# Two blocks made one, a hand-over reordered, and a two-instruction final normalisation in a one-core encoder kernel

## Chip, cores and metric

The kernel runs on one core of a Trainium2 chip. The metric is the device time of one execution in microseconds (us), lower is better. Engines are named as in the profile: PE is TensorE's matrix multiplication, PEld its weight loads, DVE is VectorE, ACT is ScalarE, POOL is GpSimd, SP is SyncE, which here only issues DMAs.

## The reference

One layer of a hybrid encoder on 16 meta tokens and 512 frames of 1024 channels, in float32:

```
h = layernorm(concat(meta, x))
p = h @ w_in                     # one projection, split among the branches
A = sparse attention: top-k keys by an indexer, attention in a 128-wide latent
    (q_abs = q . w_uk, softmax over the chosen keys, o_lat . w_uv)
B = RWKV-7 time mixing: a delta-rule scan over the tokens, 8 heads of 64
h = layernorm(alpha*h + (sigmoid(gA) * (A @ w_pa) + sigmoid(gB) * (B @ w_pb)) @ w_o)
q = h @ peer_wq                  # 8 heads x 2 halves of 128
experts = top 16 of 128 x 128 product keys per head, gates = softmax of the 16 scores
h = layernorm(alpha*h + sum over experts of gate * gelu(h . u[e]) * v[e])
```

## The kernel before

The program is a row of stages, each a block in which every engine has its own queue; engines meet by semaphores. Between two blocks all engines meet at a barrier, and the stage's semaphores are cleared.

- `project` (to about 326 us of the profile): the input norm, the projection, the choice of keys.
- `attend` (328 to 412): SP loads w_uk and w_uv at the block's start. PE turns the latent keys (line 968), multiplies the queries of eight heads by w_uk (line 976; ACT copies each result to q_abs, line 919), then for four query tiles of 128: scores (988), softmax by DVE and ACT, transposes of the probabilities (999), latent sums (1008), and `attended_of` (1017), whose result ACT copies in `take_out` (941). POOL builds the seven masks of the scan.
- `scan_chunks` (412 to 560): SP loads w_pa. DVE makes scaled keys (`make_hats`, 1166), PE turns values and keys (`turn`, 1283), then products of keys and queries (`gram`, 1299), steps of a triangular inverse (1320), and so on, for one tile of 16 tokens and four of 128.
- `join` and `peer` share one last block, from 561 us on. `join` mixes the branches and multiplies by w_o (line 1581): for each of NT = 4 tiles of 128 tokens two halves of 512 channels. DVE adds each half to h_tok (1650), takes moments (1654, 1656), ACT a root (1519, `root_of`), DVE normalises (1660). PE turns the tile before last (`turn`, 1559), ACT and DVE copy it to h1T (1528, 1636), ACT makes the high parts h_hl (1533, 1535), DVE the low parts (1643). High and low parts are the two pieces by which a float32 product is done as three fp32r products.
- `peer` streams tiles of 128 columns of weights: ACT makes the high part of each (`high`, line 1960 in the loop of heads), POOL the low part (`low`, line 1938), PE multiplies. The first two tiles are the queries of head 0; they are done in halves of 256 tokens (`query_half`, 2066 and 2070). Later tiles have 384 or 512 tokens (`tile`, 2083 and 2087). DVE ranks scores (lines 2220 to 2265) and makes gates (2273 to 2284), which PE turns (2137). POOL's queue begins with a wait for the last w_o product.
- Tokens of tiles 1 to 3 go densely through all 128 experts of each of 128 key rows (EXPERT_KEYS = 128): hidden values (2083, 2087), gelu (2040), gates (2345), high and low coefficients (2034, 2349), sums with v in PSUM (2177). The last HLS = 3 key rows are summed tile by tile. Tile 0 is gathered instead: 2 x PICKS = 256 gathered row sets, which DVE multiplies (1687) and adds (1696) between its other work; the last one is added in the turn of key row 124.
- After the loop over key rows, DVE finishes each tile: adds PSUM (2391), moments (2394, 2396), ACT's root (2050), reciprocal (2376), subtract and scale (2378), times g2 (2381), plus b2 (2383); SP stores it (1927). SP loads the rows g2 and b2 (1923, 1924) once the last low part is made.

Of the kernel before, what the change touches and what calls it, by code (L numbers as in the profile page):

```python
# [22 lines left out]
ALU = mybir.AluOpType  # L23
# [94 lines left out]
def build(nc, a, out):  # L118

    with ExitStack() as ctx:  # L120
# [17 lines left out]
        eps = sb("eps", [P, 4])  # L138

# [8 lines left out]
        with ExitStack() as layer:  # L148
# [9 lines left out]
            masks = sb("masks", [P, 7, CHUNK], at=layer)  # L158
            project(nc, a, locals())
            attend(nc, a, locals())  # L160
            w_pa = sb("w_pa", [P, PAIRS, D], at=layer)
            scan_chunks(nc, a, locals())
# [16 lines left out]
def project(nc, a, g):  # L179
# [19 lines left out]
    with ExitStack() as ctx:  # L199
# [53 lines left out]
        wi_summed, wi_taken = sem("wi_summed"), sem("wi_taken")  # L253
# [17 lines left out]
        def _(sp):  # L271
# [553 lines left out]
def attend(nc, a, g):  # L825


# [4 lines left out]
    with ExitStack() as ctx:  # L832
        sb = lambda name, shape: ctx.enter_context(nc.sbuf_tensor(name, shape, F32))
        sem = semaphores(nc, ctx, "attend")
        w_uk = sb("w_uk", [P, PAIRS, KV])
        w_uv = sb("w_uv", [P, HEADS * HD])
        cT, c_tok = p_all[:, CT_CKV, 1:PW], sb("c_tok", [P, 1 + NT, KV])
        q_abs = sb("q_abs", [P, HEADS, SEQ])
        probs = sb("prob", [P, 2, HEADS, T])
        peak, low_peak, total, share = (sb(n, [P, HEADS]) for n in ("peak", "low_peak", "total", "share"))  # L840
        probT = sb("probT", [P, 3, 4 * P])
        lat = sb("lat", [P, HEADS, P])
        landed = sem("uk_landed")
        c_turned, c_copied, abs_done, abs_copied = sem("c_turned"), sem("c_copied"), sem("abs_done"), sem("abs_copied")
        att_done, att_read, exped, shared, scaled_s, scaled_v = (
            sem(n) for n in ("att_done", "att_read", "exped", "shared", "scaled_s", "scaled_v"))
        turned, turn_copied, lat_copied, out_done, out_copied = (
            sem(n) for n in ("p_turned", "p_copied", "lat_copied", "oa_done", "oa_copied"))
        order_sem = sem("dve_order2")
        q = p_all[:, CT_Q:CT_Q + 4, 1 + META:PW]  # L850
        ones, masks = g["ones"], g["masks"]
        whole = [sb(f"mask{n}", [P, P]) for n in range(6)]
        pool_order, used = sem("pool_order4"), sem("probT_used")

        turns_before = lambda i: sum(2 * (x + 2) for x in range(i))
        units = lambda i: 2 * (i + 2)

        def heads_at(i, u):

            return range(HEADS * u // units(i), HEADS * (u + 1) // units(i)) if i + 1 < NT else range(0)  # L860

        block = ctx.enter_context(nc.Block())

        @block.sync
        def _(sp):
            sp.dma_start(w_uk[:, :, :], a["w_uk"]).then_inc(landed, 16)
            sp.dma_start(w_uv[:, :], a["w_uv"]).then_inc(landed, 16)
            sp.wait_ge(landed, 32)

        @block.gpsimd  # L870
        def _(pool):

            order = Order(pool, pool_order)
            below16, below32, below64, above16, above64, upto64 = whole

            def within(dst, w):
                view = dst[:, :].rearrange("p (b w) -> p b w", w=w)
                order.put(nc.gpsimd.affine_select(out=view, in_=ones[:, :].rearrange("p (b w) -> p b w", w=w),
                                                  compare_op=ALU.is_ge, fill=0.0, base=0,
                                                  pattern=[[-w, P // w], [0, w]], channel_multiplier=1))  # L880
                order.settle()
                order.put(nc.gpsimd.affine_select(out=view, in_=view, compare_op=ALU.is_ge, fill=0.0, base=w - 1,
                                                  pattern=[[w, P // w], [0, w]], channel_multiplier=-1))

            def side(dst, src, mult, strict):

                return nc.gpsimd.affine_select(out=dst[:, :], in_=src[:, :], compare_op=ALU.is_ge, fill=0.0,
                                               base=-strict, pattern=[[mult, P]], channel_multiplier=-mult)

            within(above16, 16)  # L890
            within(above64, 64)
            within(below32, 32)
            order.settle()
            order.put(nc.gpsimd.tensor_tensor(below64[:, :], above64[:, :], below32[:, :], ALU.subtract))
            order.settle()
            order.put(nc.gpsimd.tensor_tensor(below32[:, :], below32[:, :], above16[:, :], ALU.subtract))
            order.put(side(below16, above16, -1, 1))
            order.put(side(upto64, above64, 1, 0))
            order.settle()
# [1561 lines left out]
```

## Time and profile before

| | us |
|---|---|
| median of 3 runs | 1988.38 (1982.52 to 1988.75) |
| profiled execution, its own time | 1988.63 |
| its span in the trace | 1986.8 |
| PE busy | 1873.1 |
| DVE busy | 1540.8 |

All row times are us from the span's start. A row of the timeline has start, duration, engine, line, operation, output and inputs, shapes, and how many instructions are merged (x8); behind it in brackets the engine's idle time before it and who ended that. The profiled execution's own time is 1.83 us longer than its span.

### The profile page before, as it was taken

The page shows a single profiled execution, that of the slowest core. Times are in us where ns is not written, and L with a number is a line of the kernel's source. Part 1 is how long each engine was busy: PE and PEld are TensorE (multiplying, and loading weights), DVE is VectorE, ACT ScalarE, POOL GpSimd, SP SyncE. Part 2 cuts the span into 40 slices and gives each one's busy share as a digit, 9 for nine tenths or more (in the row PEclk, how much of TensorE's full clock was granted, in tenths as well). Part 3 has the DMA queues.
Part 4 walks back from the last instruction along what each step waited for, and adds up shares of the span by engine and source line. Part 5 has one row for each costly group of instructions (what it writes and reads, how often), then busy time and mean ns, then how long its engine had stood idle before and what let it go on. Part 6 is the DMA issues. An engine that isn't in the chain of part 4 may idle for free.

```text
span 1986.8 us, 33852 instructions
## 1 busy us (share of the span) xinstructions
PE 1873.1 (94%) x13154; PEld 1598.1 (80%) x13154; DVE 1540.8 (78%) x2833; ACT 762.5 (38%) x1114; POOL 600.8 (30%) x403
## 2 busy tenths in 40 slices
PE   6989998989999999999999999869999999999996
PEld 5978776578954589999999999858787878899995
DVE  7398992425453489999989999768788888879897
ACT  4323454732210144433456666423333333333332
POOL 2313333000000155555532222432222232345550
PEclk9989898979999999999999999979999999999998
DMA  4212231010051144344588888999999999989991
GB/s 141 75 54 75 82 109 64 1 44 4 4 212 43 51 136 137 125 138 144 160 321 324 313 315 315 335 385 357 345 349 351 353 367 354 371 302 351 366 351 64
DMA packets 173722, 416.58 MB, mean 210 GB/s; under 512 B 13952, under 2 KB 89216, under 8 KB 170384
## 3 DMA queue, kind: packets, MB, share of 16 engines
q1 hardware_dynamic: 119728, 256.16, 37.6%
q0 software_dynamic: 36864, 134.23, 17.9%
q10 hardware_dynamic: 16992, 24.26, 3.3%
q8 instruction: 98, 1.61, 0.3%
q14 instruction: 40, 0.33, 0.1%
HBM read 363.08 MB, written 51.51 MB: 209 GB/s over the span
## 4 chain that ended last, share of the span: by engine, by line
PE 47%; DVE 15%; DMA 7%; issue 1%; ACT 1%; SPq 0%; DVEq 0%; ACTq 0%
PE ps L2177 21%; PE ps L2083 11%; PE ps L2087 5%; DMA gates<-dense_gates 4%; PE ps L2150 3%; PE ps L1548 3%; PE ps L1581 3%; DVE is_place L2262 2%; DMA coef<-parked_gelu 2%; DVE is_place L2257 1%; DMA w_staged<-in_stream 1%; DVE picks L2265 1%; DVE top_at L2232 1%; DVE top_at L2223 1%; DVE s_head L2226 1%
## 5 line engine op out<-in xcount | busy, mean ns | idle before, releaser
L2177 PE MATMUL ps<-w_hl,coef_hl 128*128 128x512 f32 x2304 | 537.2, 394 | 21.1 <-DVE coef_hl L2349 21.1
L2177 PEld LDWEIGHTS ps<-w_hl,coef_hl 128*128 128x128 f32 x2304 | 433.8, 189 | 117.6 <-DVE coef_hl L2349 23.5
L2083 PE MATMUL ps<-h_hl,w_hl 128*128 128x384 f32 (+1 forms) x2272 | 436.7, 343 | 5.5 <-ACT h1T L1966 5.5
L2083 PEld LDWEIGHTS ps<-h_hl,w_hl 128*128 128x128 f32 x2272 | 398.4, 188 | 17.3 <-ACT w_hl L1998 6.1
L1677 POOL DMA_INDIRECT gathered_rows<-in_u_rows,pick_index x128 | 163.2, 1275 | 379.7 <-DVE pick_hidden L1687 359.6
L1998 ACT ACTIVATE w_hl<-w_staged 128x1024 fp32r<-128x1024 f32 x143 | 152.2, 1064 | 240.8 <-PE ps L2177 154.7
L1677 POOL DMA_INDIRECT gathered_rows<-in_v,pick_index x128 | 165.0, 1289 | 233.8 <-DVE h_tok L1696 197.1
L2087 PE MATMUL ps<-h_hl,w_hl 128*128 128x384 f32 (+1 forms) x1136 | 226.0, 340 | 0.0
L1938 POOL TENSOR_TENSOR w_hl<-w_staged,w_hl 128x1024 fp32r<-128x1024 f32 x64 | 162.1, 2534 | 139.6 <-ACT w_hl L1960 114.0
L2087 PEld LDWEIGHTS ps<-h_hl,w_hl 128*128 128x128 f32 x1136 | 200.3, 188 | 4.4
L1696 DVE SCALAR_TENSOR_TENSOR h_tok<-gathered_rows,pick_hidden,h_tok 128x1024 f32<-128x1024 f32 x128 | 164.0, 1282 | 6.3
L2318 DVE TENSOR_TENSOR w_hl<-w_staged,w_hl 128x1024 fp32r<-128x1024 f32 x130 | 158.0, 1220 | 9.7 <-ACT w_hl L1998 9.7
L311 POOL TENSOR_TENSOR w_hl<-w_staged,w_hl 128x1024 fp32r<-128x1024 f32 x40 | 100.2, 2505 | 199.9 <-ACT w_hl L515 199.9
L720 PE MATMUL ps<-hT_hl,w_hl 128*128 128x264 f32 (+1 forms) x864 | 159.9, 343 | 0.0
L720 PEld LDWEIGHTS ps<-hT_hl,w_hl 128*128 128x128 f32 x864 | 136.7, 199 | 20.8 <-ACT w_hl L515 2.4
L1687 DVE CUSTOM_DVE_ANT_0 gathered_rows<-gathered_rows,h_tok 128x1024 f32<-128x1024 f32 x128 | 153.0, 1219 | 0.0
L1998 ACT ACTIVATE w_hl<-h1T 128x1024 fp32r<-128x1024 f32 x78 | 83.0, 1064 | 177.7 <-PE ps L2177 134.0
L2345 DVE TENSOR_TENSOR coef<-coef,gates 128x384 f32<-128x384 f32 x128 | 70.9, 554 | 57.7 <-DMA gates<-dense_gates 23.1
L2349 DVE TENSOR_TENSOR coef_hl<-coef,coef_hl 128x384 fp32r<-128x384 f32 x128 | 71.1, 556 | 53.4 <-ACT coef_hl L2034 53.2
L1966 ACT ACTIVATE h1T<-ps 128x384 f32<-128x384 f32 x102 | 50.0, 491 | 154.1 <-PE ps L2087 150.1
L1933 POOL IOTA count<- 128x16 f32 x1 | 0.1, 149 | 350.9 <-PE ps L1581 350.9
L2013 ACT ACTIVATE lot<-ps 128x512 f32<-128x512 f32 x96 | 96.5, 1111 | 19.9 <-PE ps L2150 18.7
(326 smaller groups left out, 2555.2 us busy)
## 6 DMA issues: line engine op xcount, KB each, us to landing
w_staged<-in_stream SPq DMA_DIRECT2D x132, 512.0 KB, 5.3
h1T<-in_v SPq DMA_DIRECT2D x66, 512.0 KB, 7.4
w_staged<-in_v SPq DMA_DIRECT2D x62, 512.0 KB, 7.3
dense_gates<-lot SPq DMA_DIRECT2D x24, 1024.0 KB, 4.9
gates<-dense_gates SPq DMA_DIRECT2D x16, 1536.0 KB, 15.7
w_staged<-in_w_in_t SPq DMA_DIRECT2D x40, 512.0 KB, 3.3
parked_gelu<-h1T ACTq DMA_DIRECT2D x102, 192.0 KB, 3.7
coef<-parked_gelu SPq DMA_DIRECT2D x102, 192.0 KB, 6.4
```

Source lines behind the costliest of these rows:

```text
L311: nc.gpsimd.tensor_tensor(w_hl[:, j, 1, :], w_staged[:, j, :], w_hl[:, j, 0, :].bitcast(F32), ALU.subtract).then_inc(w_low, 1)
L720: nc.tensor.matmul(banks[b], w_hl[:, j, 0, P * k:P * (k + 1)], hT_hl[:, part, k, lo:hi], start=(k == 0 and part == 0), stop=False)
L1677: nc.gpsimd.indirect_dma_start(gathering["rows"][:, slot, :], None, table, bass.IndirectOffsetOnAxis(gathering["index"][:, column:column + ...
L1687: nc.vector.tensor_tensor_reduce(rows, rows, h_tok[:, 0, :], 1.0, 0.0, ALU.mult, ALU.add, gathering["hidden"][:, n:n + 1]).then_inc(gather ...
L1696: nc.vector.scalar_tensor_tensor(h_tok[:, 0, :], gathering["rows"][:, slot, :], gathering["hidden"][:, pick:pick + 1], h_tok[:, 0, :], ALU ...
L1938: nc.gpsimd.tensor_tensor(w_hl[:, j % RING, 1, :], staged[:, j % RING, :], w_hl[:, j % RING, 0, :].bitcast(F32), ALU.subtract).then_inc(w_ ...
L1998: nc.scalar.activation(w_hl[:, s % RING, 0, :], stage[place_of(s)], ACT.Copy).then_inc(w_high, 1)
L2013: nc.scalar.activation(lot[:, n % 2, :, FOUR * q:FOUR * (q + 1)].rearrange("p k n -> p n k"), ps[:, 4 + q, :].rearrange("p (n k) -> p n k" ...
L2083: nc.tensor.matmul(ps[:, bank, 0:width], w_hl[:, j % RING, 0, P * k:P * (k + 1)], h_hl[:, part, k, lo:SEQ], start=(k == 0 and part == 0), ...
L2087: last = nc.tensor.matmul(ps[:, bank, 0:width], w_hl[:, j % RING, 1, P * k:P * (k + 1)], h_hl[:, 0, k, lo:SEQ], start=False, stop=(k == KD ...
L2177: last = nc.tensor.matmul(ps[:, 2 + 2 * t + half, :], coef_hl[:, k % HLS, c, P * t:P * (t + 1)], w_hl[:, s % RING, v, 512 * half:512 * (ha ...
L2318: v_.tensor_tensor(w_hl[:, s % RING, 1, :], stage[place_of(s)], w_hl[:, s % RING, 0, :].bitcast(F32), ALU.subtract).then_inc(late_low, 1)
```

## The change

- w_uk and w_uv are loaded in `project`, into a part of h1T that is free by then; `attend` no longer waits for them. The masks' scratch lies in h1T too.
- `attend` and `scan_chunks` become one block, `attend_and_scan`. Each engine's queue holds its attention part, then its scan part, with waits on named semaphores where PSUM banks are handed over. PE does the scan's first `turn` before the attention's last `attended_of`; ACT copies the three turned tensors before the last `take_out`. w_pa is loaded at this block's start.
- `join`: the turn of tile 2 is moved into the second half of tile 3's w_o product (behind k = 1), ACT and DVE take it before tile 3's root and norm; ACT's `root_of(3)` comes behind tile 2's copies.
- `peer`: POOL's wait for the last w_o product is gone, so that the low parts of the first weight tiles can be made as soon as their high parts are. The first queries are done as 384 tokens (tiles 0 to 2) and 128 tokens (tile 3) instead of 256 and 256.
- The end: g2 and b2 go to two slots of the gather ring, loaded when the last gathered rows are used. Tile 0's moments are taken by DVE in the turn of key row 125, its first normalising instruction in that of 126 (behind a wait for g2 and b2). The normalisation has two instructions, (x - mean) * g2 and (that) * rstd + b2, the second in two halves, each stored by a DMA of its own. Sums, PSUM adds and moments of the last tile go by halves.

```diff
@@ project, on SP
+            sp.wait_ge(rows_used, 1)
+            sp.dma_start(g["w_uk"], a["w_uk"]).then_inc(uk_landed, 16)
+            sp.dma_start(g["w_uv"], a["w_uv"]).then_inc(uk_landed, 16)
...
+            sp.wait_ge(uk_landed, 32)
@@ attend, on PE
-            pe.wait_ge(landed, 32)
@@ attend_and_scan: DVE
+            attend_vector(dve)
...
+            dve.wait_ge(*attention["masks"])
             make_hats(0)
@@ ACT
+            last_output = attend_scalar(act)
...
                     nc.scalar.activation(dst[0:n, tt % 2, :], ps[0:n, bank, :], ACT.Copy).then_inc(tok_copied, 1)
+                if not tt:
+                    last_output()
@@ PE
+            last_output = attend_tensor(pe)
+            pe.wait_ge(*attention["scores"])
...
                 turn(tt)
+                if not tt:
+                    last_output()
@@ join, on ACT
-            if i + 1 < NT:
+            if 0 < i + 1 < NT - 1:
                 root_of(i + 1)
...
+            if i == NT - 2:
+                root_of(NT - 1)
@@ join, on PE
+                    if n == 2 * NT - 1 and k == 2:
+
+                        turn(NT - 2)
...
-            if i:
+            if 0 < i < NT - 1:
                 turn(i - 1)
@@ join, on DVE
+                if i == NT - 1 and half:
+                    take_turned(i - 1)
                 dve.wait_ge(wo_done, 2 * i + half + 1)
@@ peer, on SP
-            sp.wait_ge(late_low, STREAMED - BY_POOL)
+            sp.wait_ge(gathering["used"], 2 * PICKS)
...
             for t in range(NT):
-                sp.wait_ge(ready, t + 1)
-                sp.dma_start(out[0, P * t:P * (t + 1), :], h_tok[:, t, :]).then_inc(stored, 16)
+                for half in range(2):
+                    columns = slice(512 * half, 512 * (half + 1))
+                    sp.wait_ge(ready, 2 * t + half + 1)
+                    sp.dma_start(out[0, P * t:P * (t + 1), columns], h_tok[:, t, columns]).then_inc(stored, 16)
@@ peer, on POOL
-            pool.wait_ge(wo_done, 2 * NT)
@@ peer, on PE
+            def query_part(s, last_tile):
+
+                now = slice(SEQ - P, SEQ) if last_tile else slice(0, SEQ - P)
...
-            query_half(0, 0)
+            query_part(0, False)
             last_turn()
-            query_half(1, 0)
-            query_half(0, 1)
-            query_half(1, 1)
+            query_part(1, False)
+            query_part(0, True)
+            query_part(1, True)
@@ peer, on DVE
+            def centred(t):
+
+                put(v_.scalar_tensor_tensor(h_tok[:, t, :], h_tok[:, t, :], mv[:, t, 0:1], g2_row, ALU.subtract, ALU.mult))
+
+            def scaled(t):
+                dve.wait_ge(std_ready, t + 1)
+                put(v_.reciprocal(rstd[:, t:t + 1], std[:, t:t + 1]))
+                settle()
+                for half in range(2):
+                    columns = slice(512 * half, 512 * (half + 1))
+                    v_.scalar_tensor_tensor(h_tok[:, t, columns], h_tok[:, t, columns], rstd[:, t:t + 1], b2_row[:, columns],
+                                            ALU.mult, ALU.add).then_inc(ready, 1)
...
+                if k == EXPERT_KEYS - 3:
+                    dve.wait_ge(gathering["used"], 2 * PICKS)
+                    moments(0)
+                if k == EXPERT_KEYS - 2:
+                    dve.wait_ge(row_landed, 32)
+                    centred(0)
+
+            scaled(0)
```

## Rows read from the trace of the kernel before

**Rows 1.** The page: the chain that ended last, by engine.

```profile
PE 47%; DVE 15%; DMA 7%; issue 1%; ACT 1%; SPq 0%; DVEq 0%; ACTq 0%
```

**Rows 2.** The timeline from attend's first product to its wait for w_uv.

```profile
327.76 0.71 PE L968 MATMUL ps<-ident,arena 128*16 128x128 f32 x5 [2.29 <-PEq L112]
...
331.07 6.08 PE L976 MATMUL ps<-arena,w_uk 64*128 64x512 f32 x16 [2.60 <-DMA w_uv<-in_w_uv]
```

**Rows 3.** A stretch there: us, length, PE busy, granted clock, DMA share, GB/s.

```profile
335.00:336.00 1.00, 1.00 (x5) 0.71 0.00 0
```

**Rows 4.** The timeline from the attention's last sums to the scan's first products.

```profile
407.22 1.98 PE L1008 MATMUL ps<-probT,c_tok 128*128 128x512 f32 x4
...
409.88 1.09 PE L1017 MATMUL ps<-lat,w_uv 128*64 128x128 f32 x16 [0.69 <-ACT lat L936]
...
412.94 0.60 PE L1283 MATMUL ps<-ident,arena 128*16 128x128 f32 x4 [1.96 <-DVEq L1169]
...
414.54 0.55 PE L1299 MATMUL ps<-ab 64*16 64x16 f32 x16
```

**Rows 5.** The timeline around join's last tile and the first queries.

```profile
657.90 1.04 PE L1559 MATMUL ps<-ident,h_tok 128*128 128x128 f32 x8
...
660.92 0.81 DVE L1660 TENSOR_SCALAR h_tok<-h_tok,mv,rstd 128x1024 f32<-128x1024 f32 x1
...
687.32 0.69 DVE L1650 SCALAR_TENSOR_TENSOR h_tok<-h_tok,ps 128x512 f32<-128x512 f32 x1 [6.18 <-PE ps L1581]
...
689.06 7.96 POOL L1938 TENSOR_TENSOR w_hl<-w_staged,w_hl 128x1024 fp32r<-128x1024 f32 x3
...
690.14 1.83 DVE L1660 TENSOR_SCALAR h_tok<-h_tok,mv,rstd 128x1024 f32<-128x1024 f32 x1
...
693.94 3.62 DVE L1643 TENSOR_TENSOR h_hl<-h1T,h_hl 128x512 fp32r<-128x512 f32 x2 [0.70 <-ACT h_hl L1533]
...
699.54 1.29 DVE L1643 TENSOR_TENSOR h_hl<-h1T,h_hl 128x512 fp32r<-128x512 f32 x2 [0.70 <-ACT h_hl L1533]
...
700.98 3.58 PE L2066 MATMUL ps<-h_hl,w_hl 128*128 128x256 f32 x16 [4.54 <-DVE h_hl L1643]
```

**Rows 6.** The timeline of PE and DVE behind it.

```profile
708.23 2.94 PE L2083 MATMUL ps<-h_hl,w_hl 128*128 128x384 f32 x16
...
720.96 1.65 DVE L2220 MAX8 top<-s_head 128x8 f32<-128x128 f32 x8 [4.45 <-ACT s_head L1990]
```

**Rows 7.** The timeline of PE in project, fp32r products of 248 columns.

```profile
29.44 2.08 PE L686 MATMUL ps<-hT_hl,w_hl 128*128 128x248 f32 x16
```

**Rows 8.** The timeline of PE in the loop of heads, float32 passes of 128 columns.

```profile
712.39 1.95 PE L2097 MATMUL ps<-sub_keys,h1T 128*128 x16
```

**Rows 9.** A group by line and shape: count, busy us, mean ns, idle before.

```profile
L2150 PE MATMUL ps<-hot 128*128 128x128 bf16 x1152 | 74.4, 219 | 0.0
```

**Rows 10.** What PE waited for: us in total, times, longest.

```profile
PE ps L2137 <- DVE picks L2284: 3.1, 1, 3.1
...
PE ps L2177 <- DVE coef_hl L2349: 21.1, 6, 15.7
```

**Rows 11.** The timeline of the end.

```profile
1951.85 0.55 DVE L2349 TENSOR_TENSOR coef_hl<-coef,coef_hl 128x384 fp32r<-128x384 f32 x1
...
1955.67 12.52 PE L2177 MATMUL ps<-w_hl,coef_hl 128*128 128x512 f32 x54
...
1958.02 1.28 DVE L2394 BATCH_NORM_STATS2 stats<-h_tok 128x6 f32<-128x512 f32 x2
...
1959.99 1.28 DVE L2391 SCALAR_TENSOR_TENSOR h_tok<-h_tok,ps 128x512 f32<-128x512 f32 x2 [0.45 <-PE ps L2177]
...
1966.17 1.28 DVE L2391 SCALAR_TENSOR_TENSOR h_tok<-h_tok,ps 128x512 f32<-128x512 f32 x2
...
1980.78 1.23 DVE L2383 TENSOR_TENSOR h_tok<-h_tok,w_staged 128x1024 f32<-128x1024 f32 x1
```

**Rows 12.** DMA issues of the end: count, KB each, median us to landing.

```profile
w_staged<-in_ln_b SPq DMA_DIRECT2D x1, 512.0 KB, 5.1
```

More of the change, by code:

```diff
@@ new lines, in attend @@
+    turned, turn_copied, lat_copied, out_done, out_copied = (
+        sem(n) for n in ("p_turned", "p_copied", "lat_copied", "oa_done", "oa_copied"))
+    order_sem = sem("dve_order2")
+    q = p_all[:, CT_Q:CT_Q + 4, 1 + META:PW]
+    ones, masks = g["ones"], g["masks"]
+    whole = [g["flat_h1T"][:, P * n:P * (n + 1)] for n in range(6)]
+    pool_order, used, masks_made = sem("pool_order4"), sem("probT_used"), sem("masks_made")
+    with ExitStack() as first:
+        q_abs = sb("q_abs", [P, HEADS, SEQ], at=first)
+        probs = sb("prob", [P, 2, HEADS, T], at=first)
@@ L1065, in scan_chunks @@
-def scan_chunks(nc, a, g):
+                last = nc.tensor.matmul(ps[HD * e:HD * (e + 1), 7, P * j:P * (j + 1)], w_uv[:, HD * h:HD * (h + 1)],
+                                        lat[:, h, :], start=True, stop=True)
+            last.then_inc(out_done, 1)
+        scores(0, range(HEADS))
+        for i in range(NT):
+            for u in range(units(i)):
+                turn(i, u // (i + 2), u % (i + 2))
+                if u == 0 and i:
+                    attended_of(i - 1)
+                scores(i + 1, heads_at(i, u))
+                if u:
+                    latent(i, (u - 1) // (i + 2), (u - 1) % (i + 2))
+            latent(i, 1, i + 1)
@@ L1067, in scan_chunks, with attend_and_scan @@
+    free = {"scores": (att_read, HEADS * NT), "turned": (turn_copied, turns_before(NT)), "latent": (lat_copied, 2 * NT),
+            "output": (out_copied, NT), "masks": (masks_made, 1)}
+    return on_gpsimd, on_scalar, on_tensor, on_vector, free
+def attend_and_scan(nc, a, g):
     ps = g["ps"]
@@ L1326, in begin_x @@
                 pe.wait_ge(gram_read, 2 * NG * (tt + 1))
+                if not tt:
+                    pe.wait_ge(*attention["turned"])
                 if tt:
@@ L1364, in begin_state @@
                 pe.wait_ge(tok_copied, 3 * (tt + 1))
+                if not c:
+                    pe.wait_ge(*attention["latent"])
                 if c:
@@ L1396, in y_of_values @@
                     pe.wait_ge(y_read, tt)
+                if not tt:
+                    pe.wait_ge(*attention["output"])
                 for j in range(PAIRS):
@@ L1425, in _ @@
                 turn(tt)
+                if not tt:
+                    last_output()
                 for i in range(NG):
@@ L2401, in _ @@
-            normed(NT - 1)
+                if k == EXPERT_KEYS - 3:
[5 more added lines that the diff above has]
+            scaled(0)
+            for t in range(1, NT):
+                for half in range(2):
+                    if t < NT - 1:
+                        dve.wait_ge(sum_done, EXPERT_KEYS - HLS + HLS * t)
+                    else:
+                        dve.wait_ge(half_summed, half + 1)
+                    part = h_tok[:, t, 512 * half:512 * (half + 1)]
+                    put(v_.scalar_tensor_tensor(part, part, ALPHA, ps[:, 2 * t + half, :], ALU.mult, ALU.add))
+                    settle()
+                    moments(t, [half])
+                centred(t)
+                scaled(t)
```

449 lines of the change are left out of this document (205 added, 244 removed).

## Prediction

> **What bounds the kernel now.** The page came first. PE is busy for 1873.1 of the span's 1986.8 us, and the chain that ended last is PE for 47%, DVE for 15% [rows 1], so a gain must either shorten the stretches where PE stands still or shorten the end, where PE is done. The change touches five places, and I read the timeline of each: where attention begins [rows 2, 3], where it hands over to the scan [rows 4], the last tile of join with the first queries [rows 5, 6], what follows those queries [rows 10], and the end [rows 11, 12]. In all of them but the expert stage one engine waits for one other, so the terms can be added.
>
> **Start of attention.** PE turns the latent keys at 327.76, done at about 328.47, and then stands for 2.60 us because w_uv has not landed [rows 2]. The new kernel loads both matrices in project, behind the last projection tile, so this 2.60 goes. The two DMAs (256 KB each) and their issue are hidden there under PE's products, whose weights have by then all been asked for. Something more hangs on the clock. While PE stood, its clock fell to the lower level of 1.2 GHz, and the stretch from 335 to 336, with 0.71 granted on average, is the one in which it rose to 2.4 GHz again [rows 3], some 4.5 us after the products had begun; so most of their 6.08 us ran at half clock. Without the stand PE begins 2.6 us earlier and has hardly paused. If the clock comes back as long after the start as before, the gain is 2.6; if it comes back earlier, up to half of the 4.5 us at half clock is saved too, 4.5 or so in all, less what ACT's eight copies set as a pace. If on the contrary a later stretch of thin work falls to half clock that did not before, 2.0. I take 3.0: the stand and a little of the clock.
>
> **Attention to scan.** The last latent sums end at 409.20 (407.22 + 1.98). Then PE waits for ACT's copy and does the last output from 409.88 to 410.97, ACT copies it, all engines meet, DVE makes its keys, and PE turns from 412.94; the first gram is at 414.54 [rows 4]. In the new block DVE has made the scan's first keys while PE was still in the attention (they need only project's tensors and POOL's masks). PE turns at once: 1.60 us of turns (412.94 to 414.54) from 409.2 to 410.8. The last output needs ACT's copy, ready by 409.88, so it is no longer waited for: 1.09 more, gram at about 411.9, with the scores' and outputs' PSUM waits long met. Behind ACT's three copies, which gram needs, stands the last take_out, which delays ACT's first step copy by one short instruction, while PE is in its grams. Gain 414.54 - 411.9 = 2.6; without ACT in the way at most 3.2, and with half of the meeting's cost kept as new waits 1.5. I take 2.7. POOL's mask work is the same and is needed only by the scan, some 70 us later; w_pa's load moves from the scan's start to the attention's, where no other DMA is waited for.
>
> **Join's last tile and the first queries.** Four things happen here, so I lay the new order out.
> PE: the turn of a tile is 1.04, its last 0.17 under the next product, so 0.87 wherever it stands [rows 5]; inside tile 3's second half it makes that product end 0.87 later, so DVE's add starts at 688.19 instead of 687.32. The turn's input, tile 2's norm, has been ready for some 5 us, so PE does not wait for it.
> DVE and ACT: tile 2's copies and low parts, which stood between tile 3's norm and tile 3's copies, are done before. Tile 3's chain is add, moments, root, reciprocal, norm: 690.14 - 687.32 = 2.82 to the norm's start, and so it starts at 691.01. The norm took 1.83 here and 0.81 for tile 1, and the two low parts of tile 2 took 3.62 against tile 3's 1.29: the slow ones ran while POOL made three weight low parts (689.06 to 697.02) [rows 5]. Those now come some 50 us earlier, behind ACT's high parts, which `join` asks for ahead of its first root; there DVE has one add for each half product of 13.90 / 2 us on PE, so a slower add is hidden; uncovered it would cost 1 or 2. So the norm ends at 691.8.
> PE again: query 0 on 384 tokens starts at 688.0, where its low part is ready, and takes 24 instructions; the 16 in front are 2.94, less 0.14 under the next [rows 6], so 0.175 each and 4.2 in all; at 692.2 tile 3 is turned, 0.87, to 693.1; query 1 on 384 tokens to 697.2. Meanwhile DVE copies to 694.4, ACT makes the high parts to 695.9 and DVE the low parts to 696.6: ready before PE asks, so the 4.54 us of standing [rows 5] are gone, with the half clock that followed them (sixteen products took 3.58 there, against 2.08 for as many of 248 columns [rows 7]).
> Now the cost: 48 products on 128 columns. No row shows fp32r at that width. At 248 columns it is 2.08 / 16 = 0.13 us at most [rows 7]; float32 passes of 128 columns, 1.95 / 16 = 0.12 at most [rows 8]; bf16 ones 74.4 / 1152 = 0.065 [rows 9]. So 0.065 to 0.13 each, 3.1 to 6.2 in all. The float32 passes are the nearest, with the same width and weights of the same bytes; less the overlap of the last I take 0.11: 5.3.
> The Trainium skill has two rules for this, in "TensorE: Matmul & The Clock Gate". Its section on the back-to-back issue gap gives some 81 ns for a stream of weight load and matmul at 128 columns; with it the 48 would take 3.9, and the forecast would be 1.4 lower. Its section on LDWEIGHTS has the load last its columns over 1.2 GHz, 107 ns, with which they would take 5.1; no row here separates the two.
> End of the queries: 697.2 + 5.3 = 702.5, where the first 384-column expert tile began at 708.23 [rows 6]. Gain 5.7; from 4.8 (0.13 each) to 7.9 (0.065).
> Does it last? DVE ranks head 0 from 720.96, after waiting 4.45 for ACT's copy of the scores [rows 6], and that copy follows PE's tiles. DVE's work before it starts with the low parts' end, 4.2 us earlier than before, so DVE's wait is 2.9 instead of 4.45 and its start still moves by 5.7. The ranks end in the one PE wait of this stage, 3.1 us for the gates [rows 10]: both sides of it move alike.
>
> **The end.** I use the old clock. DVE's turns of the last key rows get new work. Behind 125's low coefficients (to 1952.40) come tile 0's moments, 1.28 + 0.21 and waits, to 1954.05; 126's work (0.56, 1.22 and 0.55 long, as 125's) then ends at 1956.2, 0.8 later than it did. Then DVE waits for g2 and b2. The last gathered rows are used in key row 124's turn, by 1948.1; the second DMA is issued some 0.5 later and lands 5.1 after that [rows 12], 1953.7: 2.5 us of margin, no wait. Behind this wait stand key row 127's coefficients, for which PE would wait. The first instruction of the norm is 1024 wide; half of it costs 0.64 (two of 512 take 1.28), so 1.28 to 1957.5. 127's low coefficients ended before the moments at 1958.02; now they follow a gate product (0.56) and ACT's high part (0.53) and end at 1959.1. PE wants them at 1955.67 + 2 x 1.38 = 1958.4, stands 0.8, and ends at 1969.0. Nothing waits for that, since DVE ends later.
> ACT's table load and root follow its high coefficients: root at 1960.15. DVE scales tile 0 by 1961.7, when the sums of tile 1 are there. A tile then takes: adds 1.28, moments 1.28 and 0.21, centre 1.28, reciprocal 0.15, scale 1.30, and 0.35 between them, 5.85. Before it was 6.18 (1959.99 to 1966.17), with three instructions for the norm, of which the last, 1.23, ended at 1982.01 [rows 11]. Three tiles: 1961.7 + 17.6 = 1979.3, against 1982.01: 2.7 gained. The last store is half as large: of the 4.8 from DVE's end to the span's end I take off 0.6, half of what 512 KB take at some 400 GB/s. Together 3.3; 2.0 if the halves' waits double, 4.2 if the store's fixed part shrinks too.
>
> **The sum.** 3.0 + 2.7 + 5.7 + 3.3 = 14.7. The profiled execution took 1988.63, next to the median 1988.38; 1988.6 - 14.7 = 1973.9. I say 1973.8.
>
> **Rivals.**
> *The middle takes some back.* Before the first sums PE stands 15.7 us [rows 10]. If loads there were tied to time and not to progress, the join gain of 5.7 would be lost: 1979.5. Against it: each load in that stretch is released by a semaphore that moves with the work.
> *The merged block buys nothing.* If the hand-over's waits return as waits on the named semaphores, or the thin work of the scan's first tile brings 1.2 GHz to a longer stretch, 2.7 and the clock's share go: 1977 to 1979.
> *Cheaper than I count.* Products on 128 columns at 0.065 and the clock back early at attention: 2.2 + 1.5 less, 1970.1.
> *Slower.* In the expert stage PE waited for DVE's coefficients six times, 21.1 us [rows 10]. If the shifted loads, gathers and gates meet worse, such waits grow. It must add over 21 us (14.7 + 6) to end slower by 0.3%, as much again as all six waits; at 24 the time is 1998. The order of the loads is the same, which speaks against it.
> *It does not do what it says.* If DVE in the loop waits for g2 and b2, PE and DVE both lose what lies beyond 2.5 us, and the end gains nothing from 5.8 on: 1977.2.
>
> **Chances and range.** Forecast with its bounds 0.63, middle 0.12, merged block 0.09, cheaper 0.07, late rows 0.04, slower 0.03; within 0.3% 0.02. 0.3%, 6 us, is about what a measurement of this kernel can tell from no change. Adding bounds in their rough middle gives 1969 to 1978 for the forecast; with the cases of the middle and of the block it is 1967 to 1981. Faster 0.92, same 0.05, slower 0.03.
>
> **What would show it.** No PE wait on w_uv, and scores 3 us earlier; gram less than 3 us after the last latent sums; POOL's low parts near 640 and none from 689 to 697; PE without a stand from 687 to the heads' loop, with 128-column products at 0.11; DVE's last instruction about 10 us behind PE's last. Wrong would make it: half clock over the scan, sums that wait more than 21 us, or DVE standing for row 126's g2 and b2.

## The result, and the profile of the changed kernel

| | kernel before | changed kernel |
|---|---|---|
| median of ten runs | 1988.45 us (1982.52 to 1993.90) | 1976.14 us (1971.02 to 1982.77) |
| ratio of after to before | | 0.9945, 95% interval 0.9930 to 0.9961 |
| the profiled execution | 1988.63 us | 1972.33 us, span 1970.6 |

The ratio is 10.9 us less (1988.45 x 0.0055), between 7.8 and 13.9. Forecast were 1973.8 (1967 to 1981) and 14.7 less. The time lies in the range and 2.3 us from the forecast, but the predicted gain of 14.7 lies outside the measured interval. That the time came so near is partly luck, as the experiments show.

First the page of the changed kernel, its span, PE's busy time and the chain that ended last, against [rows 1].

```profile
span 1970.6 us, 33834 instructions
...
PE 1878.3 (95%) x13154; PEld 1600.6 (81%) x13154; DVE 1536.9 (78%) x2833; ACT 761.1 (39%) x1114; POOL 600.1 (30%) x403
...
PE 51%; DVE 14%; DMA 4%; issue 1%; ACT 1%; SPq 0%; DVEq 0%; ACTq 0%
```

The span is 16.2 us shorter, but PE is busy for 5.2 us more (1878.3 beside 1873.1) with the same 13154 products. So PE stands still for less time, and the same products took longer somewhere. No term of the prediction would make that.

**Start of attention.** PE's timeline, against [rows 2], and the first scores of the kernel before; then the windows that answer to [rows 3], in which the granted clock stands behind the busy times of the engines.

```profile
327.53 0.71 PE L960 MATMUL ps<-ident,arena 128*16 128x128 f32 x5 [2.29 <-PEq L112]
328.16 5.87 PE L967 MATMUL ps<-arena,h1T 64*128 64x512 f32 x16
334.88 0.76 PE L979 MATMUL ps<-arena,q_abs 128*128 128x144 f32 x4 [0.84 <-ACT q_abs L912]
```
```profile
338.29 0.76 PE L988 MATMUL ps<-arena,q_abs 128*128 128x144 f32 x4 [1.14 <-ACT q_abs L919]
```
```profile
330.00:331.00 1.00, 1.00 (x6) 0.46 (x3) 0.00 (x0) 0.93 (x2) 0.92 (x4) 0.50 1.01 418
331.00:332.00 1.00, 1.00 (x4) 0.64 (x4) 0.00 (x0) 0.38 (x2) 0.93 (x5) 0.59 0.95 381
332.00:333.00 1.00, 1.00 (x7) 0.39 (x3) 0.00 (x0) 1.00 (x3) 0.82 (x4) 1.00 1.01 414
```

The wait for w_uv is gone. From the turn of the latent keys to the first scores it takes 7.35 us, before 10.53 (338.29 - 327.76): 3.2 gained, forecast 3.0. Of these, 2.60 is the stand, 0.2 the sixteen products (5.87 us, before 6.08) and 0.3 a shorter wait for ACT's last q_abs (0.84, before 1.14). The clock is back at 2.4 GHz at about 331.8 (0.59 granted in that microsecond), 3.7 us behind the products' start instead of 4.5. Most of the sixteen still ran at 1.2 GHz: PE also stands 2.29 us ahead of the turn of the latent keys, as before, and the clock is down from 329 on (0.50 granted).

**Attention to scan.** PE's timeline, against [rows 4].

```profile
402.19 1.98 PE L999 MATMUL ps<-probT,c_tok 128*128 128x512 f32 x4
404.00 0.60 PE L1291 MATMUL ps<-ident,arena 128*16 128x128 f32 x4
404.44 1.04 PE L1291 MATMUL ps<-ident,h1T 128*16 128x128 f32 x8
405.41 1.09 PE L1008 MATMUL ps<-lat,h1T 128*64 128x128 f32 x16
406.43 0.60 PE L1307 MATMUL ps<-ab 64*16 64x16 f32 x24
```

PE goes from the last latent sums (L999) to the turns, the last output (L1008) and the first gram (L1307) without a stand: 4.24 us from the first to the last of these starts instead of 7.32, 3.1 gained, forecast 2.7. Gram starts 8.1 earlier than before, though only 3.2 + 3.1 are terms of the change: from the first scores to the last latent sums it took 1.6 less (67.3, before 68.9), and project ended 0.2 earlier.

**Join's last tile and the first queries.** PE's timeline, against [rows 5, 6].

```profile
671.45 1.04 PE L1577 MATMUL ps<-ident,h_tok 128*128 128x128 f32 x8
...
677.07 3.34 PE L2092 MATMUL ps<-h_hl,w_hl 128*128 128x384 f32 x16
...
681.64 1.03 PE L1577 MATMUL ps<-ident,h_tok 128*128 128x128 f32 x8
682.43 3.03 PE L2092 MATMUL ps<-h_hl,w_hl 128*128 128x384 f32 x16
685.30 1.55 PE L2096 MATMUL ps<-h_hl,w_hl 128*128 128x384 f32 x8
686.69 1.90 PE L2092 MATMUL ps<-h_hl,w_hl 128*128 128x128 f32 x16
...
691.10 1.06 PE L2096 MATMUL ps<-h_hl,w_hl 128*128 128x128 f32 x8
691.99 1.27 PE L2109 MATMUL ps<-h_hl,w_hl 128*128 128x384 f32 x6
```

DVE's timeline there (tile 3's norm, L1683, and its low parts, L1664), and GpSimd's low parts of the first three weights:

```profile
680.48 0.81 DVE L1683 TENSOR_SCALAR h_tok<-h_tok,mv,rstd 128x1024 f32<-128x1024 f32 x1
...
684.77 1.29 DVE L1664 TENSOR_TENSOR h_hl<-h1T,h_hl 128x512 fp32r<-128x512 f32 x2 [1.13 <-ACT h_hl L1549]
```
```profile
624.62 6.98 POOL L1964 TENSOR_TENSOR w_hl<-w_staged,w_hl 128x1024 fp32r<-128x1024 f32 x3 [72.36 <-ACT w_hl L1986]
```

Tile 2 is turned inside the last product with w_o. GpSimd is done some 50 us before the norm, and the norm takes 0.81 instead of 1.83 [rows 5]. PE has no stand from 671.45 on, and the 48 products on 128 columns take 5.30 us (691.99 - 686.69), 0.110 each. From the first product with w_o to the first expert tile it is 72.08 us (619.91 to 691.99), before 77.80 (630.43 to 708.23): 5.7 gained, forecast 5.7.

**The end.** DVE's timeline, against [rows 11]: tile 0's moments and centring inside the last key rows, its scaling, and the first and last instructions of the tiles behind it. Then PE's last sums.

```profile
1939.57 1.28 DVE L2392 BATCH_NORM_STATS2 stats<-h_tok 128x6 f32<-128x512 f32 x2
...
1943.32 1.28 DVE L2401 SCALAR_TENSOR_TENSOR h_tok<-h_tok,mv,gathered_rows 128x1024 f32<-128x1024 f32 x1
...
1947.46 1.42 DVE L2409 SCALAR_TENSOR_TENSOR h_tok<-h_tok,rstd,gathered_rows 128x512 f32<-128x512 f32 x2
1948.79 0.68 DVE L2445 SCALAR_TENSOR_TENSOR h_tok<-h_tok,ps 128x512 f32<-128x512 f32 x1
...
1954.64 0.68 DVE L2445 SCALAR_TENSOR_TENSOR h_tok<-h_tok,ps 128x512 f32<-128x512 f32 x1
...
1965.00 1.41 DVE L2409 SCALAR_TENSOR_TENSOR h_tok<-h_tok,rstd,gathered_rows 128x512 f32<-128x512 f32 x2
```
```profile
1946.27 5.84 PE L2203 MATMUL ps<-w_hl,coef_hl 128*128 128x512 f32 x24 [0.34 <-DVE coef_hl L2384]
1951.95 4.36 PE L2222 MATMUL ps<-w_hl,coef_hl 128*128 128x512 f32 x18
```

The centring waits for no row of g2 or b2, PE stands 0.34 us, and a tile takes 5.85 us (1948.79 to 1954.64), as forecast. DVE ends 10.10 us behind PE instead of 13.82, and 23.42 us behind the start of the last sums (1942.99) instead of 26.34: 2.9 gained. From DVE's end to the span's end it is 4.2 us instead of 4.8. Together 3.5, forecast 3.3.

The four terms come to 3.2 + 3.1 + 5.7 + 3.5 = 15.5 us. The measured gain is 10.9. Something that isn't among them costs 4.6.

### The profile page after: what moved, and what is told of

Read it like the earlier page. It is cut to its first block, busy times and chain, and to the rows that moved or that the text cites. A ratio compares the mean times of both kernels' runs of the same rounds, so it can differ in the third digit from the quotient of the medians.

```text
span 1970.6 us, 33834 instructions
## 1 busy us (share of the span) xinstructions
PE 1878.3 (95%) x13154; PEld 1600.6 (81%) x13154; DVE 1536.9 (78%) x2833; ACT 761.1 (39%) x1114; POOL 600.1 (30%) x403
## 4 chain that ended last, share of the span: by engine, by line
PE 51%; DVE 14%; DMA 4%; issue 1%; ACT 1%; SPq 0%; DVEq 0%; ACTq 0%
PE ps L2203 25%; PE ps L2109 11%; PE ps L2113 5%; PE ps L2176 3%; PE ps L1566 3%; PE ps L1602 3%; DVE is_place L2297 2%; DMA coef<-parked_gelu 2%; DVE is_place L2292 1%; DMA w_staged<-in_stream 1%; DVE picks L2300 1%; DVE top_at L2267 1%; DVE top_at L2258 1%; DVE s_head L2261 1%; DMA gates<-dense_gates 1%
## 5 line engine op out<-in xcount | busy, mean ns | idle before, releaser
L2024 ACT ACTIVATE w_hl<-h1T 128x1024 fp32r<-128x1024 f32 x78 | 82.8, 1061 | 190.5 <-PE ps L2203 146.7
L2353 DVE TENSOR_TENSOR w_hl<-h1T,w_hl 128x1024 fp32r<-128x1024 f32 x78 | 94.4, 1217 | 3.0 <-ACT w_hl L2024 3.0
```

Source lines behind the costliest of these rows:

```text
L2024: nc.scalar.activation(w_hl[:, s % RING, 0, :], stage[place_of(s)], ACT.Copy).then_inc(w_high, 1)
L2353: v_.tensor_tensor(w_hl[:, s % RING, 1, :], stage[place_of(s)], w_hl[:, s % RING, 0, :].bitcast(F32), ALU.subtract).then_inc(late_low, 1)
```

## Experiments

Twelve more kernels ran. Stage lengths of all profiles, in us, each the difference of two starts or ends in PE's or DVE's timeline:

| kernel | last latent sums to first gram | first gram to join's first product | first product with w_o to first expert tile | first hot product to the last one's end | first sums to the last one's end | PE's end to DVE's end |
|---|---|---|---|---|---|---|
| before | 7.32 | 146.7 | 77.80 | 265.4 | 647.1 | 13.82 |
| changed | 4.24 | 144.4 | 72.08 | 266.6 | 648.0 | 10.10 |
| join_alone | 7.12 | 154.2 | 72.08 | 266.6 | 651.4 | 13.69 |
| tail_alone | 7.13 | 152.3 | 77.86 | 265.8 | 650.4 | 10.27 |
| block_alone | 4.24 | 144.5 | 77.82 | 265.4 | 642.2 | 13.81 |
| early_keys | 7.85 | 148.1 | 77.86 | 265.4 | 642.4 | 13.79 |
| layout_alone | 7.12 | 151.8 | 77.79 | 266.6 | 647.9 | 13.69 |
| join_home | 8.37 | 150.9 | 72.10 | 265.4 | 646.6 | 13.81 |
| after_home | 4.24 | 150.9 | 72.10 | 265.4 | 650.1 | 10.26 |
| after_other_gap | 4.24 | 144.4 | 72.10 | 266.9 | 649.8 | 10.13 |
| home_halves | 4.24 | 147.3 | 71.90 | 265.4 | 645.2 | 10.26 |
| home_latelow | 4.24 | 150.1 | 73.77 | 265.4 | 641.3 | 10.26 |
| aligned | 4.24 | 150.9 | 72.10 | 265.5 | 644.6 | 10.27 |
| gap_72k | 4.24 | 144.9 | 72.11 | 265.7 | 640.9 | 10.34 |

Counting the stages from the left, the third holds within 0.1 us wherever the code in it is the same and the sixth within 0.25, so one profile settles what a part does there. The second and the fifth don't hold, and there only the time of the whole over many runs can tell. Ratios below are to the kernel before, measured beside each.

**1. The parts one by one.** *join_alone* is the kernel before with the join and query part:

```
+                    if n == 2 * NT - 1 and k == 2:
+
+                        turn(NT - 2)
...
-        count16, count128 = sb("count16", [P, K]), sb("count128", [P, P, 2], BF16)
+        count16, count128 = g["count16"], g["count128"]
...
-            pool.wait_ge(wo_done, 2 * NT)
...
-            query_half(0, 0)
+            query_part(0, False)
             last_turn()
```

> The kernel before with the join and query part alone. Terms add: ranks of head 0 start 5.7 us earlier than in the kernel before, at about 715.3, and the whole is 5.7 shorter (ratio 0.9971). The middle takes some back: the ranks start 5.7 earlier all the same, but the first sums of the expert stage (at 1321.1 in the kernel before) move by only 2 to 3, since the DMA engines are full in front of them, and the whole is 2 to 3 shorter.

Ratio 1.0008 (0.9992 to 1.0025), 1993.19 us: nothing gained, though the stage itself is 5.7 shorter. The rival of the middle isn't what happened either: from the gates' turn (984.77) to the first sums (1322.97) it takes 338.2 us, 2.6 more than before (335.6), of which 1.2 is in the hot products and 1.5 between the gates and them, where the granted clock is 0.92 instead of 1.00. Neither is a wait for a load. The scan, ahead of everything that this kernel changes, is 7.5 longer and the sums 4.3.

*tail_alone* is the kernel before with the new end alone.

```
+                if k == EXPERT_KEYS - 3:
+                    dve.wait_ge(gathering["used"], 2 * PICKS)
+                    moments(0)
+                if k == EXPERT_KEYS - 2:
+                    dve.wait_ge(row_landed, 32)
+                    centred(0)
```

> The kernel before with the new end alone: tile 0's moments and centring inside the last key rows, two instructions for the norm, output by halves. The prediction's term: 3.3 us shorter, last sums unmoved at 1955.7, PE standing under 1 us in them, DVE's last instruction 2.7 earlier and the last store 0.6 shorter. Rival, that the rows g2 and b2 hold DVE up in the loop: PE stands for several us before its last sums and less than 1 is gained.

Ratio 0.9990 (0.9976 to 1.0004), 2.0 us less, between 4.8 less and 0.8 more. The interval holds the forecast 3.3. The profile shows the term: 10.27 instead of 13.82, and PE's last stand is 0.43.

*block_alone* is the kernel before with attention and scan in one block and the keys loaded in project; *early_keys* has only the early load:

```
+            sp.wait_ge(rows_used, 1)
+            sp.dma_start(g["w_uk"], a["w_uk"]).then_inc(uk_landed, 16)
+            sp.dma_start(g["w_uv"], a["w_uv"]).then_inc(uk_landed, 16)
```

> The kernel before with attention and scan in one block and w_uk, w_uv loaded in project. The prediction's terms: scores 3.0 us earlier, first gram 5.7 earlier, and so the end. What the trace of the changed kernel suggests instead: scores 3.4 earlier, gram 8.1 earlier (attention itself 1.6 shorter by its clock, hand-over 3.1 shorter), join 10.5 earlier. If the middle is tied to its loads, it takes 3 of this back; if the terms are carried through, the whole is 8 to 10 shorter.

> The kernel before with w_uk and w_uv loaded in project and nothing else; attention and scan keep their own blocks. The prediction's term: no wait for w_uv, scores 3.0 us earlier, gram 3.0 earlier. If the extra 1.6 us inside attention come from the clock (it returns earlier and the heads' loop falls into half clock for a shorter time), they are here too, and gram is 5.0 earlier. If they come from the merged block, gram is 3.4 earlier at most.

block_alone: ratio 0.9956 (0.9931 to 0.9982), 8.8 us less. early_keys: 0.9983 (0.9959 to 1.0008), 3.4 less, an interval that holds no gain too. So what each part is worth is read from its stage. The early load is worth its 3.1 us at the start of attention (7.40 from the turn of the keys to the scores), and no more: its gram comes 7.85 behind the last latent sums, as in the other kernels with two blocks. The hand-over of 4.24 belongs to the merging. The 1.6 us inside attention belong to neither. From the first scores to the last latent sums it takes 67.1 to 67.5 us in eleven of the fourteen profiles, with one block or two, and 68.5 to 68.9 in three, of which before's is one. The granted clock there is 0.97 or more in the eleven and 0.95 in the three: this is the clock, and it took either value in kernels of both kinds.

The three parts add up to 9.2 us (8.8 and 2.0 less, 1.6 more), near the 10.9 of the whole, though each of the three is uncertain by 3 to 5. A loss where they meet doesn't show. The loss is inside join_alone: its stage gains 5.7 and its time doesn't. That pointed to something that the join part brings along.

**2. The place of the tiles.** What the join part moves besides instructions is memory. count16 and count128 (64 + 512 bytes a partition) now stand behind eps, so h_hl, w_hl and all between lie 576 bytes higher; coef_hl and the hot tiles stay. *layout_alone* does only this:

```
         eps = sb("eps", [P, 4])
+        count16, count128 = sb("count16", [P, PEER_TOPK]), sb("count128", [P, P, 2], BF16)
...
-        count16, count128 = sb("count16", [P, K]), sb("count128", [P, P, 2], BF16)
+        count16, count128 = g["count16"], g["count128"]
```

> The kernel before with one thing of the change: count16 and count128 (576 bytes a partition) are allocated behind eps instead of among the expert stage's tiles, so that w_hl, h_hl and all between move up by 576 bytes while coef_hl stays; order and times of all instructions are those of before. What the traces suggest: with the tiles moved the 2304 products of the last stage follow each other every 232 to 233 ns all the way instead of 228.9, and those on 384 tokens are 1.7 ns slower too, so the sums last some 8 us longer than at 228.9 and the whole is 4 to 9 us slower than the kernel before. Rival, that the rhythm comes from the order of the instructions or from chance: 228.9 for most of the stage and no difference in time.

Ratio 1.0032 (1.0013 to 1.0051): 6.4 us slower (2.6 to 10.1), with not one instruction added or moved.

*join_home* and *after_home* are join_alone and the changed kernel with every tile back at its old address:

```
-        count16, count128 = sb("count16", [P, PEER_TOPK]), sb("count128", [P, P, 2], BF16)
+        count16 = wi_tok[:, 0:2, :].rearrange("p i h -> p (i h)")
+        count128 = ones[:, :].bitcast(BF16).rearrange("p (k two) -> p k two", two=2)
...
         count16, count128 = g["count16"], g["count128"]
+        hold = sb("hold", [P, 144])
```

> The join and query part alone, as in join_alone, but with count16 and count128 as views of wi_tok and ones, which nothing reads any more by then, so that every other tile has the address it has in the kernel before. If the place of the tiles took the gain back: products of the sums at 228.9 ns, and the whole 5 to 6 us faster than the kernel before (1983 to 1984 beside 1989), where join_alone gained nothing. If the middle took it back by its loads: no difference from join_alone, 0 to 2 us slower than before.

> The whole change, with count16 and count128 as views of wi_tok and ones and every other tile of the expert stage at its old address. If the place took some back: sums at 228.9 ns a product, 640 to 642 us from the first to the last instead of 648, and the whole at 1968 to 1970, 19 to 21 below the kernel before. If it did not: 1976, as the changed kernel.

join_home: ratio 0.9960 (0.9940 to 0.9979), 8 us less, where join_alone gained nothing. after_home: 0.9901 (0.9873 to 0.9928), 19.7 us less and 1973.13 us; its interval lies just below that of the changed kernel (0.9930 to 0.9961). By the medians it is 16.1 below the kernel before (1989.18) and 3.0 below the changed kernel, so the size of the difference is loose. Expected were 1968 to 1970, and the median is 3 to 5 higher.

How it shows in the traces: windows of 90 us in the last stage without a stand of PE, counting only the line of the sums. Behind the window's length the columns are PE busy with the number of products, PE's weight loads with theirs, the granted clock, the DMA share and GB/s. First layout_alone, then after_home, then the kernel before in two places.

```profile
1330.00:1420.00 90.00, 90.00 (x389) 72.96 (x388) 1.00 1.00 352
1530.00:1620.00 90.00, 90.00 (x389) 72.99 (x388) 1.00 1.00 352
```
```profile
1600.00:1690.00 90.00, 90.00 (x395) 73.85 (x394) 1.00 1.02 362
```
```profile
1330.00:1420.00 90.00, 90.00 (x387) 72.89 (x386) 1.00 1.00 347
1535.00:1625.00 90.00, 90.00 (x395) 73.85 (x394) 1.00 1.02 363
```

At the same clock, 388 weight loads start in 90 us with the moved tiles and 394 without: a product every 232.0 or 228.4 ns. (The starts of the single products, over long stretches, give 232.4 and 228.9.) The changed kernel has 388 too, join_alone 386. The kernel before has both: 386 up to PE's first stand in this stage, at 1425.84, and 394 from there on; join_home does the same, and the other profiles at that layout have 228.9 from the first row. Over 2304 products 3.5 ns are 8 us. Not all of it reaches the end, since a faster PE catches up with DVE's coefficients. PE's waits for them, layout_alone and after_home (total, times, longest):

```profile
PE ps L2178 <- DVE coef_hl L2350: 14.8, 3, 13.4
```
```profile
PE ps L2205 <- DVE coef_hl L2386: 21.4, 7, 13.7
```

The longest comes ahead of the first sums; the others sum to 1.4 us at the slower pace and 7.7 at the faster. The stage is on average 3.8 us longer in the four profiles with moved tiles (649.3; 647.9 to 651.4) than in the nine with the old distance (645.5; 641.3 to 650.4). The ranges overlap, and after_home is itself the exception: 650.1, where 640 to 642 were expected. Its products do have the faster pace, but PE stood for 7.6 us inside the stage. So the pace is shown by the counts, and its price by layout_alone's ratio, not by the length of this stage in one profile. The hot stage adds 1.2 (266.4 to 266.9 beside 265.4 to 265.8): of its products on 384 tokens, the sixteen in front of each tile follow each other every 181.1 ns on average instead of 179.4. Together 5.0, and 6.4 measured for the whole.

*after_other_gap* is after_home without the `hold` line, so coef_hl is 576 bytes lower and w_hl at home; *aligned* has `lead = sb("lead", [P, 8])` behind eps; *gap_72k* has `hold = sb("hold", [P, 416])`.

> As after_home, but without the 576 bytes held free among the expert stage's tiles, so that w_hl and h_hl are at their old addresses and coef_hl and the hot tiles are 576 bytes lower: the distance from w_hl to coef_hl is that of the changed kernel. If the distance sets the rhythm, 232 to 233 ns a product; if the address of w_hl does, 228.9.

> after_home with 32 bytes more behind eps, so that every large tile starts on a multiple of 64 bytes instead of 32 beyond one; the distances between tiles stay. If the distance from w_hl to coef_hl sets the rhythm: 228.9 ns a product as in after_home, 1973. If the place within 64 bytes does: another rhythm, and a time at least 3 us away.

> after_home with 1088 bytes more held free among the expert stage's tiles, so that coef_hl lies 73728 bytes behind w_hl (72 times 1024) instead of 72640. If any distance but the old one is slow: 232 to 233 ns a product and 1976 to 1978. If slow and fast distances alternate, either rhythm, and a third one (faster than 228.9, with more waits for DVE's coefficients) isn't excluded.

One run of after_other_gap took 1975.77 us; its windows have 388 and 386 loads in 90 us. With w_hl at its old address and coef_hl moved it has the slow pace, so the address of w_hl alone isn't the cause. aligned: ratio 0.9903 (0.9875 to 0.9931), 1970.43 us, 394 loads. The place within 64 bytes changes nothing. gap_72k: ratio 0.9893 (0.9839 to 0.9948), 1967.84 us, and a third pace:

```profile
1590.00:1680.00 90.00, 90.00 (x399) 74.53 (x398) 1.00 1.03 369
```

398 in 90 us, 226.7 ns a product. It holds up to about 1729; from there on, where tiles of 384 tokens come between the sums, it is 229.1, as in after_home. So with w_hl to coef_hl at 72064 bytes (reached in two ways) the pace is 232 to 233 ns, at 72640 it is 228.9, but for the first rows of two kernels, and at 73728 it is 226.7 over the first hundred key rows. That stage is the shortest of all (640.9), but home_latelow's, at 228.9 ns, is hardly longer (641.3), and the kernel's interval overlaps after_home's: a gain from the third pace isn't shown.

**3. What pays in the join part.** Two kernels, one run each.

*home_halves* is after_home with `query_half` on 256 and 256 tokens in place of `query_part`:

> after_home with the first two queries in equal halves of 256 tokens again, everything else of the join part as changed. From the first product with w_o to the first 384-column expert tile it takes 77.8 us in the kernel before and 72.1 with the whole join part. By the prediction's prices: both first halves are done 1.4 us before the last tile's low parts (696.6), then 48 products on 256 columns at 0.13 us, 0.3 us later than with parts of 384 and 128: 72.4. Rival, that the uneven split is what pays: PE stands for several us for the last tile's low parts and loses its clock, 75 or more.

71.90 us from the first product with w_o to the first expert tile, 0.2 less than with 384 and 128, and less than either expectation. PE's timeline has two short stands, at tile 3's turn and at its low parts:

```profile
685.54 1.09 PE L1578 MATMUL ps<-ident,h_tok 128*128 128x128 f32 x8 [0.86 <-DVE h_tok L1684]
...
690.17 2.15 PE L2094 MATMUL ps<-h_hl,w_hl 128*128 128x256 f32 x16 [0.68 <-DVE h_hl L1665]
```

They cost less than the narrow products do: in the changed kernel 24 on 128 columns take 2.65 us (5.30 / 2) and 24 on 384 take 4.26 (682.43 to 686.69), so a third of the width costs 62% of the time. The one run took 1971.05 us.

*home_latelow* is after_home with `pool.wait_ge(wo_done, 2 * NT)` restored:

> after_home with GpSimd's wait for the last product with w_o restored, so that the three low parts of the first weights are made beside the last tile's norm again. If they slow DVE there as the prediction read it (norm 1.83 instead of 0.81, low parts 3.62 instead of 1.29) and the split of the queries covers 0.5 of it: 74 to 75 us from the first product with w_o to the first expert tile, and PE waits for the weights' low parts as well, which by the kernel before end at 697.0. Rival, that the slowness was DVE's own: 72.1 as before.

73.77 us, 1.7 more, a little under the 74 to 75 expected; the one run took 1976.56 us. PE's and DVE's timelines there:

```profile
692.47 1.66 PE L2099 MATMUL ps<-h_hl,w_hl 128*128 128x384 f32 x8 [1.40 <-POOL w_hl L1967]
```
```profile
691.14 1.83 DVE L1684 TENSOR_SCALAR h_tok<-h_tok,mv,rstd 128x1024 f32<-128x1024 f32 x1
```

The norm is back at 1.83 with GpSimd beside it (its low parts run from 690.06), so that reading held. But what PE stands for is GpSimd's low part itself, 1.40 us, not DVE.

## Why the prediction was right, and where it was wrong

- *Start of attention, 3.0.* Measured 3.2, and 3.1 in early_keys with nothing else changed: the stand of 2.6 and a little more, as taken. Only its reason for hoping for more was wrong: PE has not "hardly paused" there, since the 2.29 us ahead of the turns stay, and the clock fell all the same.
- *Attention to scan, 2.7.* Measured 3.1, by the mechanism foretold, and only with the block merged. The rival that the merging buys nothing fell: no wait came back on the named semaphores: the hand-over is 4.24 in eight profiles.
- *Join and queries, 5.7.* Measured 5.7, and the 48 narrow products at 0.110 us as priced. The Trainium skill's "TensorE: Matmul & The Clock Gate", section "LDWEIGHTS (loading the stationary operand)", has a weight load last its columns over 1.2 GHz, an estimated 107 ns for 128. The spacing of these products is near it (110), though no run shows that the load sets it. The 81 ns of the Trainium skill's section "Back-to-back issue gap" on the same page isn't what this stream does. Within the 5.7 the uneven split has no share (-0.2) and the early low parts have 1.7. The other 4.2, what is left of 5.7 + 0.2, is the turn of tile 2 inside the last product together with the order of ACT and DVE that goes with it; these two weren't tried apart. DVE begins its ranks 16.1 us earlier (704.82, before 720.96), as the first expert tile does (16.2), and waits 0.89 for ACT's scores instead of 4.45. The forecast had 2.9 there; the waits differ, but the start moves with PE as it said.
- *The end, 3.3.* Measured 3.5, with no wait for g2 and b2 and the tile at 5.85.
- *The middle takes some back.* From the first expert tile to the first sums the changed kernel's profile gives back 3.4 us (616.3 beside 612.9), which looks like this rival. It isn't its mechanism. 1.2 is the place of the tiles. 1.6 is the clock behind the gates' turn (0.92 granted, before 1.00), which join_home and early_keys show too (23.4 and 24.6 us from there to the first hot product, at 0.92 and 0.87, before 21.85) and block_alone and home_halves don't (21.8, at 1.00). The rest, 0.6, is within what this stretch varies. In join_home, with the tiles at home, the gain of join reached the end.
- *The term that was missing.* The prediction follows what GpSimd's early low parts do in time, but gives no price to the memory that they made necessary: count16 and count128 moved, and w_hl with them. That step was left out of the sum. It costs 6.4 us by itself (2.6 to 10.1).
- *What hid the miss.* 15.5 - 6.4 = 9.1, and 10.9 was measured, within its interval of 7.8 to 13.9. The forecast's 14.7 lay outside that interval, and the time came within 2.3 us of 1973.8 because the medians differ by 12.3, more than the ratio's 10.9. With the tiles at home the gain is 19.7 (14.3 to 25.3), which holds the four terms' 15.5. Whether anything lies beyond them isn't settled. The scan is a candidate: it takes 147.2 us on average in the eight profiles with one block and 150.7 in the six with two, though nothing in it changed, and both groups spread over 6 us or more.

That spread goes with the clock. Over the whole scan the granted clock is 0.92 in the three profiles with 144.4 to 144.5 us, 0.86 in the five with 150.9 to 152.3 and 0.85 in the longest, 154.2. Two windows of the scan in the changed kernel, then in after_home:

```profile
430.00:450.00 20.00, 18.67 (x503) 17.28 (x500) 7.58 (x19) 6.38 (x17) 0.00 (x0) 0.98 0.01 3
450.00:470.00 20.00, 19.25 (x627) 18.59 (x625) 10.76 (x27) 5.43 (x13) 0.00 (x0) 1.00 0.01 3
```
```profile
430.00:450.00 20.00, 19.51 (x444) 18.49 (x443) 6.75 (x17) 4.78 (x13) 0.00 (x0) 0.74 0.01 2
450.00:470.00 20.00, 18.54 (x535) 17.79 (x532) 9.54 (x25) 5.24 (x12) 0.00 (x0) 0.91 0.01 3
```

The same code does 503 and 627 products at a granted clock of 0.98 and 1.00, or 444 and 535 at 0.74 and 0.91: the second scan is 6.5 us longer (150.9 beside 144.4). Why the clock was granted so differently isn't shown. Two profiles of this kernel can differ by that without any change, so a gain of a few us can't be read from spans.

## What to carry to other kernels

An edit that frees an engine often moves a tile. Keep the addresses of the tiles that the longest stage reads, or test the new layout by itself before any of the gain is put down to the order of the work. Compare stages that the edit doesn't touch, and count instructions in windows of equal length: a few more or fewer at the same clock tell what busy shares hide. Then take each part off again and read the stage it acts in; here one of the parts, the uneven split, turned out to buy nothing.

## What the runs showed of the hardware that wasn't expected

- TensorE's products of one stage, fp32r on 512 columns with a new weight load each, at a granted clock of 1.00: 233.3, 232.4, 228.9 or 226.7 ns from start to start on average. The distance between the streamed tile (w_hl) and the tile of the weights (coef_hl) goes with it, and an offset of both by 32 bytes doesn't. The Trainium skill's "TensorE: Matmul & The Clock Gate", section "Wait — 56ns, not 53.3ns?", has back-to-back products at 2.4 GHz start every columns over 2.4 GHz plus 2.5 ns, an estimated 215.8 for 512 columns; in this stage no run came below 226.7. Why the distance matters stays open: h_hl and the hot tiles moved with the two in part, and other engines read and write SBUF in the same microseconds.
- The pace is kept like a state. The kernel before and join_home ran 24 key rows at 233.3 and changed to 228.9 at PE's first stand; after_other_gap changed from 232.4 to 233.3 at one and back at another, and join_alone from 233.3 to 232.4. gap_72k changed without a stand, from 226.7 to 229.1, where tiles of 384 tokens came between the sums.
- VectorE's norm of 1024 columns takes 0.81 us with GpSimd idle (the changed kernel) and 1.83 with GpSimd's low parts beside it (home_latelow). The prediction had read as much from [rows 5]; putting the wait back shows it.
